# Attention heads of a two-layer encoder run as one software pipeline over score tiles, with the scaling of P on GpSimd

## What is computed

```
s = q @ k.T * scale + bias          # 1024 x 1024 per head, in tiles of 128 queries
p = softmax(s, axis=-1)             # exp(s - max), divided by the row's sum
o = p @ v
```

## Time and profile before

| | us |
|---|---|
| median of 3 runs | 3236.41 (3233.12 to 3236.43) |
| span of the profiled execution | 3236.5 |
| TensorE matmuls busy in it | 2955.4 |
| VectorE busy | 1586.8 |
| ScalarE busy | 1111.6 |
| GpSimd busy | 710.7 |

### The profile page before, as it was taken

The page is one execution under the profiler, slowest core; times in us unless marked ns, Lnnn a source line. Parts: engine busy times, 40 slices in busy tenths (PEclk is TensorE's granted clock), DMA queues, the critical chain, the costliest instruction groups (busy, mean ns, idle before and its releaser), DMA issues.

```text
span 3236.5 us, 42169 instructions
## 1 busy us (share of the span) xinstructions
PE 2955.4 (91%) x14200; PEld 2381.7 (74%) x14200; DVE 1586.8 (49%) x2457; ACT 1111.6 (34%) x1827; POOL 710.7 (22%) x450
## 2 busy tenths in 40 slices
PE   6888898888899999999987888888898999999997
PEld 2677776666678888888765777777775888888885
DVE  4755565565243233223348777777714332323235
ACT  2655555554110000000135777777702001000101
POOL 1111101103423223332310000000323323332331
PEclk8999999999899999999998999999999999999998
DMA  3111111113111111111121111111221111111111
GB/s 132 60 49 37 50 44 38 37 37 130 45 38 47 52 45 45 52 48 49 52 66 45 37 37 36 36 37 41 78 100 39 46 45 52 52 45 45 52 45 52
DMA packets 195091, 167.79 MB, mean 52 GB/s; under 512 B 35258, under 2 KB 181042, under 8 KB 194226
## 3 DMA queue, kind: packets, MB, share of 16 engines
q1 hardware_dynamic: 183370, 140.05, 14.2%
q10 hardware_dynamic: 11680, 27.24, 2.6%
HBM read 146.03 MB, written 21.23 MB: 52 GB/s over the span
## 4 chain that ended last, share of the span: by engine, by line
PE 76%; DVE 8%; ACT 7%; issue 7%; DMA 1%; ACTq 1%; DVEq 1%; POOL 0%; SPq 0%; POOLq 0%
PE psS L481 15%; PE psS L483 15%; PE psS L482 15%; PE psS L549 5%; PE psD L651 5%; PE psD L647 5%; PE psD L649 5%; PE psD L579 5%; PE psD L566 4%; ACT xT L795 2%; DVE psD L953 2%; DVE pt L1016 2%; DVE rstd L948 1%; DVE hT L960 1%; PE psD L502 1%
## 5 line engine op out<-in xcount | busy, mean ns | idle before, releaser
L481 PE MATMUL psS<-hT,W 128*128 128x512 f32 x2208 | 868.4, 393 | 48.1 <-DVE hT L960 21.7
L482 PE MATMUL psS<-hT,W 128*128 128x512 f32 x2208 | 862.7, 391 | 0.0
L483 PE MATMUL psS<-hT,W 128*128 128x512 f32 x2208 | 862.1, 390 | 0.0
L393 POOL CAST W<-stage 128x1024 fp32r<-128x1024 f32 (+1 forms) x185 | 193.1, 1044 | 1806.4 <-PE psS L483 1144.1
L481 PEld LDWEIGHTS psS<-hT,W 128*128 128x128 f32 x2208 | 416.3, 189 | 149.9 <-issue 23.8
L483 PEld LDWEIGHTS psS<-hT,W 128*128 128x128 f32 x2208 | 416.5, 189 | 87.3
L482 PEld LDWEIGHTS psS<-hT,W 128*128 128x128 f32 x2208 | 416.7, 189 | 85.4 <-issue 1.0
L395 POOL TENSOR_TENSOR W<-stage,W 128x1024 fp32r<-128x1024 f32 (+1 forms) x185 | 442.4, 2391 | 14.8
L1103 DVE TENSOR_TENSOR row<-psS,row 128x512 f32<-128x512 f32 x88 | 60.9, 692 | 739.9 <-PE psS L483 739.9
L566 PE MATMUL psD<-flip_t,xT 128*128 128x128 f32 x1856 | 272.2, 284 | 70.7 <-DVE pt L1016 57.2
L1016 DVE TENSOR_TENSOR pt<-psD,pt 128x512 fp32r<-128x512 f32 (+2 forms) x512 | 301.6, 629 | 44.0 <-ACT pt L784 41.9
(11 more groups left out here) (104 smaller groups left out, 2494.1 us busy)
## 6 DMA issues: line engine op xcount, KB each, us to landing
stage<-in_w_gate SPq DMA_DIRECT2D x44, 512.0 KB, 3.8
stage<-in_w_up SPq DMA_DIRECT2D x44, 512.0 KB, 3.8
stage<-in_w_down SPq DMA_DIRECT2D x44, 512.0 KB, 3.6
xT<-rel_c SPq DMA_DIRECT2D x16, 960.0 KB, 4.5
stage<-in_w_even SPq DMA_DIRECT2D x24, 512.0 KB, 5.6
park<-xT ACTq DMA_DIRECT2D x2, 4096.0 KB, 13.9
heads<-o_out ACTq DMA_DIRECT2D x128, 64.0 KB, 1.9
xT<-park ACTq DMA_DIRECT2D x4, 2048.0 KB, 11.1
```

The source lines that it names most:

```text
L481: pe.matmul(o, wop(0, k), rhs(0, k, h), start=n == 0, stop=False)
L482: pe.matmul(o, wop(0, k), rhs(1, k, h), start=False, stop=False)
L483: mm = pe.matmul(o, wop(1, k), rhs(0, k, h), start=False, stop=n == len(ks) - 1)
```

## The change

The three attention loops are written out in full as two pipelines: one of 128 tiles over the 8 pairs of layer 0 and one of 128 tiles over the 8 pairs of layer 1. Only the first pair's projections stand ahead of each. The next pair's projections are cut into pieces, and TensorE issues a piece in a round between the scores of tile t+1 and the transposes of tile t-2: in layer 0 six products of 512 tokens, each in two parts of 12 matmuls (rounds 5 to 15 of a pair and round 0 of the next); in layer 1 eight products of 3 or 9 matmuls. All pieces go to one PSUM bank, `ps_p`. Their high and low parts are written by ScalarE and VectorE in the round after (`even_evict`, `c_evict`).

The scaling of a tile is issued by GpSimd for all tiles (`normalise`, a tensor_scalar). Tables `mneg`, `den` and `rden` have four columns for two. k and q have three sets of buffers for two, the transposed tiles three slots (`PT[..., t % 3, :]`), the products with v one PSUM bank (`ps_o`) for two, the weights two slots for three in attention. SyncE rather than ScalarE issues the DMAs of the results, and the bias tables of layer 0's second group are built in rounds 3 and 10 of a pair. Of the last pair in a pipeline, GpSimd splits the first four projected tiles in rounds 8 to 14.

The core of the diff:

```diff
+            for t in range(TILES + 5):
+                pair, step = t // NSTEP, t % NSTEP
+                if t < TILES:
+                    bias_scores(0, t, window_even, t < TILES // 2)
+                if t and filler_even(t - 1) and filler_even(t - 1)[2] and filler_even(t - 1)[1] < 4:
+                    even_evict(*filler_even(t - 1)[0:2])
+                if step in (3, 4) and pair < PAIRS:
+                    keep_v_lo(0, pair, step - 3)
+                if 2 <= t < TILES + 2:
+                    keep_p_lo(0, t - 2, window_even)
+                if t < TILES:
+                    reciprocals(0, t)
+                if t >= 5 and t % 2 == 1:
+                    sum_o(0, (t - 5) // 2)
+                if step == 10 and 3 <= pair < PAIRS - 1:
+                    build_b(2 * pair + 2)
+                if step == 3 and 4 <= pair < PAIRS:
+                    build_b(2 * pair + 1)
...
+            def normalise(t0, t, window):
+
+                s = score(t)[:, 0:window(t)[1]]
+                pool.wait_ge(S["recip"], t0 + t + 1)
+                pool.tensor_scalar(s, s, rden[:, t % 4:t % 4 + 1], 1.0, ALU.mult, ALU.mult).then_inc(S["normed"], 1)
...
+            def even_product(pair, n, part):
+
+                c, h = n // 2, n % 2
+                if part == 0:
+                    pe.wait_ge(S["ws"], at("even", "ws", 2 * (3 * pair + c) + 2))
+                    if pair:
+                        if n == 0:
+                            pe.wait_ge(S["v_lo"], 2 * pair)
+                        elif n < 3:
+                            pe.wait_ge(S["k_lo"], 8 * pair + 4 * n)
+                        elif n < 5:
+                            pe.wait_ge(S["q_lo"], 4 * pair + 2 * (n - 2))
+                        else:
+                            pe.wait_ge(S["v_row"], 2 * pair + 1)
...
+STEPS_C = {0: 0, 1: 1, 2: 2, 4: 3, 5: 4, 6: 5, 8: 6, 9: 7}
...
+            for n in (2, 3, 0, 1, 4, 5, 6, 7):
+                c_product(0, n)
```

More of the change, by code:

```diff
@@ L301, in early_heads, with store_head @@
+            def store_head(t0, g):
+                pair, e, c = g // 8, g // 4 % 2, g % 4 * 256
+                sp.wait_ge(S["o_sum"], t0 // 2 + g + 1)
+                sp.dma_start(heads[pair * P + e * HD:pair * P + (e + 1) * HD, c:c + 256], o_out[:, g % 2, :])\
+                    .then_inc(S[f"od{g % 2}"], 16)
+            def early_heads(ph, t0, tiles):
                 for b in range(2):
[L302 to L303 removed]
+                    sp.wait_ge(S[f"od{b}"], 16 * (t0 // 4 + 4 * (tiles[-1] + 1)))
+                for j in tiles:
@@ L457, in _ @@
             pool.wait_ge(S["sc"], at("attn_c", "sc", 0))
-            with pool.Fori(0, NC_PAIRS, 1) as it:
-                split("attn_c", 0, 0, ("sc", 4 - 20, 20), it, 1, dmas=8, buf=0, swap=swap_rotary)
-            pool.wait_ge(S["sc"], at("proj_1", "sc", 4 - 20))
+            for half in range(2):
+                latent_split(0, half)
+            for t in range(TILES):
+                pair, step = t // NSTEP, t % NSTEP
+                normalise(TILES, t, window_c)
+                if pair < PAIRS - 1 and step in (1, 3):
+                    latent_split(pair + 1, step // 2)
+                if pair == PAIRS - 1 and step in (8, 10, 12, 14):
+                    split_heads("proj_1", (step - 8) // 2)
             proj_weights("proj_1")
@@ L612, in _, with scores @@
-            even_phase("attn_a", "norm_a0", a_window, SEQ)
-            even_phase("attn_b", None, b_window, BW)
-            def proj(ph):
+            def scores(t0, t, window, operands):
+                k0, nk, _ = window(t)
+                if t >= 2:
+                    pe.wait_ge(S["biased"], t0 + t - 1)
+                q0 = t % QB * P
+                ops = operands(t // QB)
+                for c in range(0, nk, HALF):
+                    w = min(HALF, nk - c)
+                    for n, (q, k) in enumerate(ops):
+                        mm = pe.matmul(psS[t % 2][:, c:c + w], q[:, q0:q0 + P], k[:, k0 + c:k0 + c + w],
+                                       start=n == 0, stop=n == len(ops) - 1)
+                mm.then_inc(S["scored"], 1)
@@ new lines, in _ @@
+            for n in range(8):
+                c_evict(0, n)
+            for t in range(TILES + 5):
+                pair, step = t // NSTEP, t % NSTEP
+                if t and filler_c(t - 1):
+                    c_evict(*filler_c(t - 1))
+                if step in (3, 4) and pair < PAIRS:
+                    keep_v_hi(TILES, pair, step - 3)
+                if t < TILES:
+                    exp_scores(TILES, t, window_c)
+                if 2 <= t < TILES + 2:
+                    keep_p_hi(TILES, t - 2, window_c)
+                if t >= 5 and t % 2 == 1:
+                    keep_o_lo(TILES, (t - 5) // 2)
```

917 lines of the change are left out of this document (501 added, 416 removed).

## The result

The changed kernel takes 3413.0 us (3411.8 to 3413.8, 4 runs) against 3236.4 (3233.1 to 3240.7, 4 runs) of the kernel before: 1.0541 times as long, 95% interval 1.0526 to 1.0556. The forecast was 3389 in a range of 3280 to 3470. The profiled execution spans 3412.0 us, 175.5 more than before.

The account below looks back on a forecast made before the run. VectorE was taken to bound the kernel before inside a pair (3.24 us a tile). Layer 0 +22, layer 1 +87 and TensorE's clock +44 gave 153 on 3236.5: 3389 us, range 3280 to 3470.

Parts of the forecast that it names:

- What bounded the kernel before: Inside a pair of attention, VectorE's own work fills each tile's 3.24 us and is the bound.
- The chain from tile to tile: Bias, exp, p_hi, p_lo, next bias in series across ScalarE and VectorE: two tiles take 8.94 us, against 3.24 each.
- The waits of the pieces: Pieces share one PSUM bank and wait for low parts: k rounds 9.8 us, q 8.4; pairs attn_a 93.2, attn_c 88.7.
- attn_b: Layer 0's second group: links scaled by width, table builds 4.3 us, port 0.5, so 81.7 us per pair against 78.6.
- The clock: TensorE drops towards 1.2 GHz after idle times: 22 us at layer 0's k pieces, 22 in attn_c, together +44.
- Each issued rounds before it is needed: 0: Result DMAs join those of tables and weights on SyncE's queue and cost 0.
- The start: Before layer 0's tiles: first scores at 115 us instead of 116, as v's transposes no longer stand ahead.
- Contention of the table builds: The tables' 16 VectorE operations with both inputs in SBUF meet GpSimd: 0.25 us each on average, 4 in all.
- GpSimd's scaling: Scaling a tile on GpSimd takes between 1.05 and 2.40 us, nearer 1.05, and costs nothing at either end.
- A: Rival: pieces hide, as TensorE finds their low parts written; -65 us, 3172; chance 13%.
- B: Rival: even the chain is shorter, tiles at the busiest engine's work, 78, 66 and 64 us a pair; 3035; chance 5%.
- C: Rival: TensorE's clock falls at every wait of over 1.3 us, 99 us for 44; 3444, up to 3460; chance 14%.

Follow-up runs that it names:

- run 10: Kernel before, with GpSimd scaling all of P, weight splits in halves between scalings and head splits between the last pair's scalings: 3243.3 us, 1.0007.
- run 1: Changed kernel with ScalarE copying the high parts of tile t-2 before the exp step of tile t, both layers: 3413.6 us, 1.0539 to before.
- run 3: Changed kernel with two edits: high parts before exp on ScalarE, and TensorE's piece last in its round: 3217.8 us, 0.9933 to before.
- run 12: Version of run 8 with one edit undone, ScalarE again taking the exp step before the high parts: 3197.8 us, 0.9869 to before.
- run 8: Version of run 7 plus early output projection weights and layer 0's pieces (and splits of v's weights) one round later: 3103.8 us, 0.9585.
- run 4: Changed kernel with unused matmuls on TensorE in waits for low parts, before layer 0's k pieces and one layer 1 q piece: 3391.2 us, 1.0467.
- run 5: Changed kernel with each output projection's first two weight tiles fetched and split early in the layer's last pair: 3402.7 us, 1.0501 to before.
- run 6: Kernel before with GpSimd alone scaling all of P, whole splits of weights between the scalings: 3289.3 us, 1.0151.
- run 7: Version of run 3 plus the low half of o copied and the sum of o made first in their round: 3161.0 us, 0.9760.

## Why the prediction was right, point by point

The forecast came 22.5 us short on the span of 3412.0: by the table's rows -7.1, +12.2, +6.3, +3.5 and +7.6 us.

**What bounded the kernel before** was half right. VectorE was nearly full between two bias steps, but it wasn't the bound alone: run 10 took its scaling away, 0.75 us in two tiles, and pairs of attn_a took 92.65 us for 92.57. The forecast doesn't rest on this, since it counts the scaling that leaves VectorE as worth nothing.

**The chain from tile to tile** was right to some 0.1 us: 4.28 to 4.42 in even rounds and 4.60 in odd ones for 4.30 and 4.64. Runs 1, 3 and 12 show the part that the prediction didn't have: its order on ScalarE is worth 0 us beside the pieces' waits, 69 with the piece last and 94 in run 8's version.

**The waits of the pieces** were right: rounds with k that kept their clock took 9.82 and 9.87 us for 9.8, with q 8.55 for 8.4. A low part of 512 took 0.71 for 0.70. A pair of attn_a at full clock (run 4) took 94.1 for 93.2. In attn_c a pair took 92.15, or some 90.2 with the rotary round at full clock, for 88.7. Over a bare round its five slower ones took 2.9, 3.1, 3.4, 5.9 (7.8 less the clock) and 3.1 us, for 1.7, 3.1, 3.3, 6.0 and 3.1; before the fourth TensorE stood idle 7.15 us, for "some 7".

**attn_b** was too short by some 8 us over three pairs: 88.8, 88.8 and 85.3 for 81.7 and 3.2 of clock. The scaling by width isn't the reason: less the low clock (6.0 us in k rounds and the two items below, 6.6 and 4.0) the three pairs come to some 246 us for 245. What the sum lacked is the clock in the round behind a table build. The build holds VectorE for 2.1 us, as forecast; then TensorE's q piece waits 4.05 to 4.06 us, where the next q piece waits 2.41, and all its 12 matmuls run 0.43 us apart:

```profile
645.96 0.77 PE L707 MATMUL psD<-hT,W 128*128 128x512 f32 x1 [4.05 <-DVE kq L1220]
```

That round takes 10.0 us for 7.8, once in each of these pairs. In two of them the round after v's low parts is slowed as well, 6.5 and 7.4 us for 4.9. attn_a's last pair, too, was 4.7 over its neighbours in run 4 (98.8 for 94.1): the first of the tables are built there, and I had put all of them in attn_b.

**The clock** was 44 in the sum. At the two places that I had named it came to 29: the slowed k rounds of layer 0 make 16 for my 22, and in attn_c a slowed rotary round cost 12.20 - 10.28 = 1.9, 13 in all, for the 3.1 that I took from 24 score matmuls, too many for a piece of 9. Run 4 gave back 22. But the low level shows at places for which the sum had nothing, too: the four q pieces behind a table build (12 matmuls in 5.26 us three times and 4.08 once, for 2.83), the round after v's low parts in three pairs (8.1 us for 6.2 in attn_a, and the two above), together some 14; and the second k piece of attn_c in all seven pairs, behind an idle time of 4.27, three matmuls 0.43 apart and the transposes behind them 0.21 apart: an estimate of 8, the 2.9 above less the forecast 1.7. So at all these places the clock cost some 52 us, and that my 44 came near is partly luck: too much at the places that I had looked at, nothing at the others.

**"Each issued rounds before it is needed: 0"** was the step that was wrong in kind. It holds inside the pipeline and fails at its end: in SyncE's queue the first weights of the output projection stand behind the last result, which is the last thing that attention makes. Run 5 takes both away: 10 us by the medians, and in its profile 14, all that the table shows there.

**The start** brought 8 us, where I had put 1. Half of it is a contention that I hadn't looked for: GpSimd's first splits come earlier and in halves, and the norm's operations with two inputs in SBUF no longer meet them. Before, then after:

```profile
60.88 2.34 POOL L395 TENSOR_TENSOR W<-stage,W 128x1024 fp32r<-128x1024 f32 x1
60.88 4.33 DVE L953 SCALAR_TENSOR_TENSOR psD<-xT,gain,rstd 128x512 f32<-128x512 f32 x2
```

```profile
59.61 1.42 DVE L1134 SCALAR_TENSOR_TENSOR psD<-xT,gain,rstd 128x512 f32<-128x512 f32 x2
```

The reciprocal ahead of these rows starts at 57.49 before and 56.22 after, that of the norm's second half at 76.61 and 71.16: so 4.2 us go between them, which is what the contended operations took too long (2.89, 1.53 and 2.13 us for 0.76). 1.3 us had gone before, for a reason that I haven't found, and 2.6 go behind, where v's transposes no longer stand ahead of the first scores. I had looked for this contention only among attention's own operations. No run tries the start alone.

**Contention of the table builds** was put at 4 us, and the builds took 1.07 and 1.08 us, as in the kernel before (1.08 to 1.09): 0 on VectorE. GpSimd paid instead; see the last section.

**GpSimd's scaling** took 1.13 us for 1024 columns and TensorE's transposes wait for it 3.7 us in all in the changed kernel; on the kernel before, with half splits, it comes to nothing together with the lighter VectorE (run 10). That whole splits would cost the changed kernel what they cost in run 6 wasn't tried.

**The rivals.** A (pieces hide, 3172) and B (3035) were excluded by the rounds; but with four lines reordered, runs 7 and 8 pass A's time, so A's time is within reach of this structure. C (clock at every wait of over 1.3 us) is excluded: 6 of 14 k rounds kept it, and so did all seven q pieces of attn_a behind idle times of 1.7 us.

## What to carry to other kernels

In a pipeline whose order is written by hand, follow one item through all engines and add up the links; then list which other waits lie beside each link, since here a link was worth nothing until they were gone. A filler piece belongs behind everything that the main chain waits for, and the sharing of a buffer (here the second bank of the product with v) has to be priced as a ring of its own. When work moves to another queue, look at the pipeline's ends as well as its middle.

## What the hardware showed that I had not expected

**Who pays for contention.** GpSimd's scaling of 768 columns took 0.90 to 0.91 us alone, and beside two table builds on VectorE 2.58 to 3.00. Two of the eight places in the changed kernel:

```profile
552.34 1.07 DVE L1231 TENSOR_TENSOR xT<-xT,rstd 128x896 f32<-128x896 f32 x1
552.52 2.58 POOL L496 TENSOR_SCALAR xT<-xT,rden 128x768 f32<-128x768 f32 x1 [1.26 <-DVE rden L1181]
553.33 1.09 DVE L1233 TENSOR_TENSOR xT<-xT,rstd 128x896 f32<-128x896 f32 x1
```

```profile
510.82 2.99 POOL L496 TENSOR_SCALAR xT<-xT,rden 128x768 f32<-128x768 f32 x1 [0.22 <-DVE rden L1181]
510.96 1.07 DVE L1231 TENSOR_TENSOR xT<-xT,rstd 128x896 f32<-128x896 f32 x1
```

In all eight VectorE lost nothing, and GpSimd ended 0.7 to 0.9 us behind the second build. At 60.88 in the kernel before it was the other way round: GpSimd's subtraction took its usual 2.34, and VectorE's two operations 4.33 for 1.42. The Trainium skill, SBUF — State Buffer, section SBUF: two separate sides, says that the one that starts first has the shared ports for its whole instruction and the other is blocked. That one side pays in full agrees with every row. Which side it is doesn't follow from the recorded starts: in four of the eight places, as at 510.82, GpSimd had started 0.13 to 0.15 us ahead and paid all the same, while the 42 long operations of the earlier trace rows each started 0.13 us behind a subtraction on GpSimd, and there VectorE paid. Starts on GpSimd are rough in this profile, so the rule may hold for a moment that the rows don't show.

GpSimd's loss isn't quite free: behind the scaling stands a half split of weights. Three of the four q pieces behind a build waited last for that split, 11.9 us in all, though q's low parts, the other thing that they wait for, were written only 0.1 to 0.2 us earlier.

**The same idle time, either clock.** Of the 14 k pieces of the changed kernel 5 began at the low level, after idle times of 2.53 to 3.35 us, and 9 at the full one, after 2.53 to 3.07; three of these fell to the low level within the piece. Two of those that kept one level throughout:

```profile
256.80 0.77 PE L707 MATMUL psD<-hT,W 128*128 128x512 f32 x1 [3.07 <-DVE kq L1216]
257.37 0.63 PE L708 MATMUL psD<-hT,W 128*128 128x512 f32 x1
...
339.23 0.47 PE L707 MATMUL psD<-hT,W 128*128 128x512 f32 x1 [3.06 <-DVE kq L1216]
339.53 0.40 PE L708 MATMUL psD<-hT,W 128*128 128x512 f32 x1
```

So a price per wait is at best a mean over such cases; what sets which one it is stays open here.
